# A decoder layer on one core: 16 more tokens take their first-kind expert products from gathered rows, and a fifth group of experts is worked early

## The reference, cut to what matters

```
q = h @ w_q                                   # 8 heads, two halves of 128
s = q . sub_keys                              # 128 scores for each half
top_v, eidx = best 16 of all pairs of halves  # 8 x 16 = 128 experts a token
gw = softmax(top_v)
a = gelu(h . exp_u[eidx])                     # first kind of product
out = sum over the 128 of (gw * a) * exp_v[eidx]   # second kind
```

## Time and profile before

| | |
|---|---|
| median of 3 runs | 1888.95 us (1888.36 to 1889.47) |
| the profiled execution: time, span | 1888.78 us, 1887.0 us |
| PE busy | 1846.1 us, 98% of the span |
| DVE busy | 1468.0 us, 78% |
| ACT busy | 857.3 us, 45% |
| POOL busy | 348.4 us, 18% |
| DMA | 548.22 MB, mean 291 GB/s |

### The profile page before, as it was taken

The page is one execution under the profiler, slowest core; times in us unless marked ns, Lnnn a source line. Parts: engine busy times, 40 slices in busy tenths (PEclk is TensorE's granted clock), DMA queues, the critical chain, the costliest instruction groups (busy, mean ns, idle before and its releaser), DMA issues.

```text
span 1887.0 us, 25880 instructions
## 1 busy us (share of the span) xinstructions
PE 1846.1 (98%) x10392; PEld 1620.4 (86%) x10392; DVE 1468.0 (78%) x1953; ACT 857.3 (45%) x1152; POOL 348.4 (18%) x216
## 2 busy tenths in 40 slices
PE   7999999999899999999999999999999999999997
PEld 6888888888778999997779889889889899898895
DVE  6544655576763798968898988988888989989887
ACT  5443556344533103335555455455455455455452
POOL 1000223000000000013331323232323222323210
PEclk9999999999989999999999999999999999999999
DMA  9644333846254776789999999999999999999882
GB/s 346 237 179 179 134 135 106 321 176 245 90 201 156 240 272 226 292 309 339 370 365 364 388 360 358 393 359 366 384 345 381 382 352 393 360 354 393 346 330 98
DMA packets 100199, 548.22 MB, mean 291 GB/s; under 512 B 8704, under 2 KB 33344, under 8 KB 35952
## 3 DMA queue, kind: packets, MB, share of 16 engines
q1 hardware_dynamic: 53424, 374.37, 52.5%
q0 software_dynamic: 20096, 147.04, 19.0%
q10 hardware_dynamic: 26560, 25.17, 4.3%
HBM read 530.74 MB, written 14.68 MB: 289 GB/s over the span
## 4 chain that ended last, share of the span: by engine, by line
PE 94%; DVE 3%; ACT 1%; issue 1%; DMA 0%; SPq 0%; POOL 0%; DVEq 0%; ACTq 0%
PE bank L954 16%; PE bank L581 11%; PE bank L598 9%; PE bank L855 8%; PE bank L956 7%; PE bank L887 6%; PE bank L890 6%; PE bank L886 6%; PE bank L888 6%; PE bank L889 6%; PE bank L583 6%; PE bank L875 2%; PE bank L821 1%; DVE rows L1730 1%; DVE oh L1829 1%
## 5 line engine op out<-in xcount | busy, mean ns | idle before, releaser
L581 PE MATMUL bank<-act_split,ring_hi 128*128 128x512 f32 x896 | 319.1, 399 | 10.9 <-DVE ring_lo L1362 8.2
L1840 DVE TENSOR_TENSOR split_a<-experts,split_a 128x2048 fp32r<-128x2048 f32 x124 | 283.8, 2288 | 53.5 <-ACT split_a L1277 52.8
L1351 DVE TENSOR_TENSOR ring_lo<-ring_raw,ring_hi 128x2048 fp32r<-128x2048 f32 x90 | 205.9, 2290 | 137.9 <-ACT ring_hi L1017 137.5
L1277 ACT CAST split_a<-experts 128x2048 fp32r<-128x2048 f32 x124 | 237.3, 1914 | 147.6 <-PE bank L890 146.4
L954 PE MATMUL bank<-h_split,split_a 128*128 128x384 f32 x1024 | 293.9, 359 | 0.2 <-DVE hres L1904 0.2
L956 PE MATMUL bank<-h_split,split_a 128*128 128x192 f32 x1024 | 256.3, 250 | 0.0
L583 PE MATMUL bank<-act_split,ring_lo 128*128 128x256 f32 x896 | 252.0, 281 | 0.0
L555 POOL DMA_INDIRECT rows<-in_peer_u,eidx x64 | 148.0, 2312 | 455.2 <-DVE rows L1730 452.0
L555 POOL DMA_INDIRECT rows<-in_peer_v,eidx x64 | 148.1, 2314 | 374.4 <-DVE hrow L1736 328.6
L581 PEld LDWEIGHTS bank<-act_split,ring_hi 128*128 128x128 f32 x896 | 169.5, 189 | 50.2 <-DVE act_split L1362 8.0
L1017 ACT CAST ring_hi<-ring_raw 128x2048 fp32r<-128x2048 f32 x90 | 171.8, 1909 | 83.3 <-PE bank L598 73.7
(11 more groups left out here) (295 smaller groups left out, 3457.9 us busy)
## 6 DMA issues: line engine op xcount, KB each, us to landing
experts<-in_stream SPq DMA_DIRECT2D x218, 1024.0 KB, 5.2
ring_raw<-in_stream SPq DMA_DIRECT2D x91, 1024.0 KB, 4.8
late_raw<-in_stream SPq DMA_DIRECT2D x38, 1024.0 KB
gate_matrix<-stage ACTq DMA_DIRECT2D x12, 1024.0 KB, 4.9
gbuf<-gate_matrix ACTq DMA_DIRECT2D x16, 768.0 KB, 13.3
w<-in_w SPq DMA_DIRECT2D x4, 1024.0 KB, 8.6
gb<-in_ln_g POOLq DMA_DIRECT2D x3, 1024.0 KB, 4.9
gb<-in_ln_b POOLq DMA_DIRECT2D x3, 1024.0 KB, 9.2
```

The source lines that it names most:

```text
L581: pe.matmul(bank[n % 2][:, :], hi[:, k * P:(k + 1) * P], act_split[:, k].rearrange("p c t -> p (c t)"), start=(k == 0), stop=False, skip_g ...
L1277: act.copy(split(m)[0], tile).then_inc(split_hi, 1)
L1351: dve.tensor_tensor(ring_lo[:, r, :], ring_raw[:, r, :], ring_hi[:, r, :].bitcast(F32), ALU.subtract).then_inc(lo_ready, 1)
L1840: dve.tensor_tensor(lo, raw_slot(split_slot(m))[0], hi.bitcast(F32), ALU.subtract).then_inc(split_lo, 1)
```

## The change

- `NU = 176`: the first-kind products of the early and of the late groups are made for 176 tokens in place of 192 (early 128x176; late 128x352 and 128x176). The second kind stays dense for 192.
- The other 16 tokens (176 to 191) get their first-kind products from 16 more gathers (`FIRST`; 16 x 128 rows), which stand first. They are used in the first 32 quads of the choice. Their dot products (`bpair`) get gelu on ACT at quad 33, go back by 8 small DMAs from POOL into a tile of ones (`spread_b`), and DVE multiplies them into the softmax weights at quad 38; PE transposes those again at quad 39, and ACT copies the 16 columns that changed. In `early_chunk` and `ga` the last 16 columns are set to 1 once, so that gelu(product) x gate leaves the gate for them.
- `EARLY_G = 5`: 40 early slots and 11 late groups. PE does 6 early steps a quad for 32 quads and 4 for the other 16.
- Four buffers of one-hot tiles in place of two (`HOTS`).
- Gathers: 16 during the choice, 2 while loading, 22 in V0, 10 in each late group, 4 of them in its first half.
- The first loads: x in quarters as before, but the first two weight slots in a first quarter and a rest, with the rest ahead of x's third and fourth quarter.
- The split tokens are made at chunk 31 in place of 24, and the gathered tokens' gelu at the end of its group's second half.

```diff
-EARLY_G = 4
+EARLY_G = 5
...
+NU = 176
+NB = ND - NU
+EIGHTHS = P // NB
+FIRST = PAIRS // EIGHTHS
...
+HOTS = 4
...
-STEP = 3
-CHOICE_S = 8 * EARLY_G - QUADS * STEP // KO - WHILE_LOADING
+STEPS = [6] * 32 + [4] * 16
+CHOICE_S = 8 * EARLY_G - sum(STEPS) // KO - WHILE_LOADING
+GELU_N, BACK_N, TURN_N, WEIGHTED_N = 33, 38, 39, 44
-IN_G, IN_LOADING, IN_V0, IN_LATE = 6, 2, 17, 9
-IN_LATE_U = 3
+IN_G, IN_LOADING, IN_V0, IN_LATE = FIRST, 2, 22, 10
+IN_LATE_U = 4
...  sync: the first loads
+            quarter_of_x(0)
+            for r in range(2):
+                sp.dma_start(ring_raw[:, r, 0:512], a["stream"][r][:, 0:512]).then_inc(first_landed[r], 16)
+            quarter_of_x(1)
+            for r in range(2):
+                sp.dma_start(ring_raw[:, r, 512:], a["stream"][r][:, 512:]).then_inc(landed[r], 16)
+            quarter_of_x(2)
+            quarter_of_x(3)
...  gpsimd
+            for e in range(EIGHTHS):
+                pool.dma_start(eidx_b[e * NB:(e + 1) * NB, :],
+                               eix[NU - P:NS, e * FIRST:(e + 1) * FIRST]).then_inc(eidx_landed, 16)
+            for n in range(FIRST, FIRST + 2 * GATHERS):
+                pool.wait_ge(row_used, n - BUFS + 1)
+                if n == FIRST + BUFS - 1:
+                    for half in range(2):
+                        pool.dma_start(hrow[half * NS:(half + 1) * NS, :], hres[NS:P, 1, :]).then_inc(hrow_landed, 16)
+                    pool.wait_ge(spread_ready, 1)
+                    pool.wait_ge(bpair_gelu, 1)
+                    for e in range(EIGHTHS):
+                        pool.dma_start(spread_b[NU - P:NS, e * FIRST:(e + 1) * FIRST],
+                                       bpair[e * NB:(e + 1) * NB, :]).then_inc(bpair_landed, 16)
...  tensor
-                    last = pe.matmul(bank[(N_U + k) % 2][:, 0:ND], experts[:, k % RP, ko * P:(ko + 1) * P], h2T[:, ko, :],
+                    last = pe.matmul(bank[(N_U + k) % 2][:, 0:NU], experts[:, k % RP, ko * P:(ko + 1) * P], h2T[:, ko, 0:NU],
...
+                if n == TURN_N:
+                    pe.wait_ge(weighted_ready, 1)
+                    pe.transpose(bank[2][:, 0:P], pick[:, 1, 2].rearrange("p h k -> p (h k)"), ident[:]).then_inc(idx_psum, 1)
...
-                            pe.matmul(b[:, 0:2 * ND], hi[:, w], h2_split[:, ko].rearrange("p c t -> p (c t)"), start=(ko == 0),
+                            pe.matmul(b[:, 0:2 * NU], hi[:, w], h2_split[:, ko].rearrange("p c t -> p (c t)"), start=(ko == 0),
...
-                            last = pe.matmul(b[:, 0:ND], lo[:, w], h2_split[:, ko, 0, :], start=False, stop=(ko == KO - 1),
+                            last = pe.matmul(b[:, 0:NU], lo[:, w], h2_split[:, ko, 0, :], start=False, stop=(ko == KO - 1),
...  scalar
+                if n == GELU_N:
+                    act.wait_ge(row_used, FIRST)
+                    act.activation(bpair[:], bpair[:], ACT.Gelu_apprx_tanh).then_inc(bpair_gelu, 1)
+                if n == TURN_N:
+                    act.wait_ge(idx_psum, TT + 1)
+                    act.copy(idxT[:, 2, NU:ND], bank[2][:, NU - P:NS]).then_inc(idx_out, 1)
...  vector
             for n in range(QUADS):
-                if n >= 2:
-                    dve.wait_ge(g_mm, n - 1)
+                if n >= HOTS:
+                    dve.wait_ge(g_mm, n - HOTS + 1)
+                if n == BACK_N:
+                    dve.wait_ge(spread_ready, 1)
+                    dve.wait_ge(bpair_landed, 16 * EIGHTHS)
+                    weights = pick[0:NS, 1, 2].rearrange("p h k -> p (h k)")
+                    dve.tensor_tensor(weights, weights, spread_b[0:NS, :], ALU.mult).then_inc(weighted_ready, 1)
+                if n == WEIGHTED_N:
+                    dve.wait_ge(idx_out, TT + 1)
...
-                gathers(IN_CHOICE + (IN_G - IN_CHOICE) * (n + 1) // QUADS)
+                gathers(min(IN_G, IN_G * (n + 1) // 32))
```

More of the change, by code:

```diff
@@ L275, in early_chunk @@
             flat = early[:].rearrange("p c t -> p (c t)")
-            first = 32 * T - N_EARLY * ND
-            return flat[:, first + k * ND:first + (k + 1) * ND]
+            return flat[:, k * ND:(k + 1) * ND]
         def raw_slot(n):
@@ L318, in build @@
         landed = [sem(f"landed{r}") for r in range(R)]
-        first_landed = [[sem(f"first_landed{r}{q}") for q in range(3)] + [landed[r]] for r in range(2)]
+        first_landed = [sem(f"first_landed{r}") for r in range(2)]
         first_hi = sem("first_hi")
@@ L434, in _, with quarter_of_x @@
         def _(sp):
[L435 to L436 removed]
+            def quarter_of_x(q):
+                k = slice(4 * q, 4 * q + 4)
                 sp.dma_start(act_raw[:, k, :], a["xT"][:, k, :]).then_inc(x_landed[q], 16)
[L438 to L439 removed]
+            quarter_of_x(0)
[6 more added lines that the diff above has]
+            quarter_of_x(3)
             for s in range(2, R):
@@ L874, in _ @@
                 for j in range(QUAD):
-                    last = pe.matmul(bank[4 + n % 4][:, j * P:(j + 1) * P], oh2[:, n % 2, j, :], oh1[:, n % 2, j, :],
+                    last = pe.matmul(bank[4 + n % 4][:, j * P:(j + 1) * P], oh2[:, n % HOTS, j, :], oh1[:, n % HOTS, j, :],
                                      start=True, stop=True)
                 last.then_inc(g_mm, 1)
-                for step in range(STEP * n, STEP * n + STEP):
+                if n == TURN_N:
+                    pe.wait_ge(weighted_ready, 1)
+                    pe.transpose(bank[2][:, 0:P], pick[:, 1, 2].rearrange("p h k -> p (h k)"), ident[:]).then_inc(idx_psum, 1)
+                for step in range(sum(STEPS[:n]), sum(STEPS[:n + 1])):
                     early_slot(CHOICE_S + step // KO, (step % KO, step % KO + 1))
@@ L962, in _ @@
                         for ko in range(KO):
-                            last = pe.matmul(b[:, 0:ND], tile[:, ko * P:(ko + 1) * P], h2T[:, ko, :], start=(ko == 0),
+                            last = pe.matmul(b[:, 0:NU], tile[:, ko * P:(ko + 1) * P], h2T[:, ko, 0:NU], start=(ko == 0),
                                              stop=(ko == KO - 1))
@@ L1743, in gathers @@
                 nonlocal seen
-                while seen < min(upto, 2 * GATHERS):
+                while seen < min(upto, FIRST + 2 * GATHERS):
                     gathered(seen)
```

97 lines of the change are left out of this document (58 added, 39 removed).

## The result

Six runs of the changed kernel have a median of 1878.43 us (1876.39 to 1879.41), six of the kernel before on the same chips 1889.21 us. The ratio is 0.9941, 95% interval 0.9928 to 0.9954: faster, by 0.6% or 11 us. The forecast was 1861.9 us, 27 us faster; the measured time lies inside its range of 1849 to 1879, near the upper end, and the gain is less than half of the forecast one. The profiled execution has a span of 1877.3 us against 1887.0.

What follows compares the result with a forecast made beforehand. PE's work was taken to set the time, with DMA close behind. PE's work -29.3, choice -2.8, transpose, copy and wait +1, and DMA +4 summed to -27.1 us: 1861.9 us as a median, range 1849 to 1879.

Steps and rivals of the forecast that it cites:

- V0: Stage V0: 8 chunks more at 4.60 us each, its 512-column matmuls unchanged, +36.8 us.
- Two cost 1.03 us and landed 1.7 us after: Way back of the 16 products in the choice: 5.8 us to issue and land, DVE waiting 1 to 3, unseen by PE.
- Rival 5: In the choice, the way back stalls PE by 10 us, with POOL's issues slowed: 1872 us; chance 0.05.
- rival 2: DMA becomes the bound at a 0.98 share, late groups +17 us, choice losing 8: 1879.9 us; chance 0.14.
- Early slots: Early slots at 149.7 ns a record, 4.79 us a slot, 40 in place of 32: +25.2 us.
- The pair at its floor, 271 ns: Late groups' first halves: only the wide matmul shrinks, 12.8 ns less a pair, 1.64 us a group.
- Rival 4: Late groups' pair is set by its two weight loads and doesn't shrink at all: 1875.9 us; chance 0.06.
- the bound where both shrink: Late groups: both matmuls of a pair shrink by their columns, 19.2 ns a pair, late groups -100.3 us.
- DMA, +4 us: Late groups: 71.8 us of transfers in PE's 71.6, costing 0.4 us in each of 10 groups, between 0 and 17.
- rivals 2 and 3: Rival 3: late groups' transfers go no faster than now, a group taking 76.0 us: 1902 us; chance 0.06. Rival 2: own line.
- The choice: Choice: PE and DVE run level, 3 us lost where 5 to 5.8 were: -2.8 us; extra transpose, copy, wait: +1.
- Start: First loads reordered at the kernel's start: 0 us, between -1 and +2.

Runs made afterwards that it cites:

- e1: The changed kernel with the 8 way-back DMAs issued ahead of the copies of hrow and of gathers 16 and 17 in POOL's queue: 1871.32 us.
- e2: The changed kernel without the 8 way-back DMAs and DVE's wait for them, leaving the 16 tokens' first-kind products out of its result: 1864.63 us.
- e3: The changed kernel with its three new small tiles moved behind the one-hot tiles, so w_split lies where it was before: 1869.45 us.
- e11: The kernel of e9_best with w_split alone 128 bytes higher: 1866.67 us.
- e12: The kernel of e9_best with w_split at its place and wt, gbuf and ga 128 bytes higher: 1861.90 us.
- e8: The kernel before with the fifth early group alone (EARLY_G = 5, STEP = 5, IN_V0 = 26, split tokens at chunk 29): 1889.01 us, ratio 0.9995.
- e9_best: The changed kernel with DVE's multiplication at quad 42, PE's transposes behind quad 41 and w_split at its address of before, POOL's order left: 1860.44 us.
- e7: The changed kernel with the narrow matmul of each late pair at 128 columns in place of 176: 1876.23 us.
- e4_back42: The changed kernel with DVE's multiplication at quad 42 in place of 38 and PE's transposes behind quad 41 in place of 39: 1867.15 us.

## Why the prediction was wrong

The direction it forecast was right, and so were PE's terms to within 2 us, but for V0's; the size was 27 us where 11 were measured. Two steps failed.

*"Two cost 1.03 us and landed 1.7 us after, so 4.1 + 1.7 = 5.8 us. DVE waits 1 to 3 us ... so PE doesn't see it."* The issues cost what was said, 4.28 us for eight. The landing did not: it took 11.4 us. The 1.7 us came from the indices' DMAs of the earlier trace rows, which were two of 16 KB, not eight of 1 KB, and stood in POOL's queue before any gather. Eight of 1 KB took 3.8 us even there, as the change's own indices show. On the way back they stood behind two gathers and the two copies of `hrow` (which the prediction had itself put there, and costed as POOL's time alone), while the DMA share was 1.01. e1 took both away, what was ahead and most of the traffic, and came to 4.6 us; the two were not tried apart. The rest of the passage held: DVE came to quad 38 at 820.80, and PE ran out of work 4.7 us later (834.98 - 9.46 = 825.52), the "some 5 us" of the forecast. e2 shows the price, 11.8 us before V0, of which 9.5 is idle and the rest the slower clock behind it. Rival 5 had this mechanism with its 10 us and a chance of 0.05, but for a wrong reason, slow issues.

*"V0 ... all matmuls of 512 columns, which the change leaves: +36.8."* The change left the matmuls and moved their stationary tile: three new small tiles were allocated in front of w_split. e3, e11 and e12 show that its place costs 1.3 us in V0 and 5.3 behind it, 6.6 in all. Nothing in the rows of before could have said so, but that an address moves could be read in the kernel. Of the 2.4 us that V0 missed, the other 1.1 are not the address: e8, with w_split at its place of before, also took 185.0/40 = 4.63 us a chunk and not 4.60. Why was not followed.

With the stall hidden and the address put back the forecast is met: e9_best has 1860.4 us where 1861.9 were forecast. That it comes so near is in part luck. Against the terms of the forecast it has 0.9 us more before V0, 1.1 more in V0 and 1.5 more in the late groups than PE alone was given, and the 4 us set down for DMA didn't come. It is luck too that the change itself, at 1878.4, fell inside the range and beside rival 2's 1879.9: rival 2's signs are not in its profile, where ACT waited for no slot in the late groups and DVE 0.7 us in all for rows.

The other terms, point by point:

- *Early slots* at 150 ns a record: PE's quads in the choice and the 239.2 us of e2 bear it out. The forecast had 23.4 more than before in that stretch, e2 has 239.2 - 216.0 = 23.2.
- *The pair at its floor, 271 ns*: 273 measured, so 11.2 ns less than before and not 12.8, and 1.43 us a group, not 1.64. e7 shows the floor: 48 columns fewer of the narrow matmul give at most 2.6 us of 27. That the floor is the weight load stays an argument, from the weight-load row that is busy all through the first halves. Rival 4 (no shrinking at all) is out, and so is the bound where both shrink.
- *DMA, +4 us*: nothing. At shares of 0.97 to 1.00 in ten late windows PE had no wait for a slot. With w_split in its place the late groups with the end gave 898.0 - 808.3 = 89.7, of 91.3 for PE alone. The queue could be kept full; rivals 2 and 3 had the right quantity (71.8 us of transfers in 71.6) and the wrong consequence. The Trainium skill's 358 GB/s (DMA: Bandwidth & Descriptors, section Where 436 GB/s comes from) is passed by ten of the eleven late windows, at 384 to 398 GB/s (the last has few gathers) on this one core.
- *The fifth group*: priced by the same rows at +5.1 less what PE loses in the choice, 0 to 3 expected, 0 measured. So nothing of the gain is from it by itself; that it makes room for the quads' new work is its purpose, and wasn't tried apart.
- *The choice* without the way back: of e2's 239.2 us, 190.5 are 1280 early records at 149 ns, 42.7 the quads and 0.9 the transposes; 5 are left as lost, where the forecast took 3 and 1. Its PE waited 2.0 us for one-hot tiles.
- *Start*: +0.6 in the change's profile, between -2.8 and +1.3 over all profiles, so no effect that can be told.

## What to carry to other kernels

A small transfer that something waits for can't be priced by the landing of another one in an emptier stage (1.7 us there, 11.4 here): look at the number and size of the transfers, at what is ahead of them in their own queue at that moment, and at the DMA share of that stage. Put its consumer far behind it before trying to make it faster; that was worth 10.3 us of the stretch before V0 (e4_back42), the faster landing 6.8 (e1_queue). When new tiles are allocated, look whether a stationary operand of many matmuls has moved, and if matmuls that the change doesn't touch start further apart, move it back and measure. A DMA share near 1.0 is not by itself a bound on PE: here, with rings of three to five buffers, it took nothing from PE. With shorter rings it was not tried.

## What the runs showed of the hardware

- The spacing of back-to-back matmuls of 512 columns depends on where the stationary tile lies: with w_split 216 bytes past a multiple of 256, 230.7 ns in every kernel with five early groups; 88 past one (at 182872 and at 182360), 232.6 to 232.8 ns; at a multiple of 256, 233.3 ns. That is 1% of a stage, 5 to 7 us of this kernel. Why, and what the best place is, stays open: three residues were tried. The place is not all of it: the kernel before has the 216 too, and 229.4 ns in V0.
- Eight DMAs of 1 KB, counted from the last issue to the wait's end, took 3.8 us with nothing ahead in their queue (DMA share 0.58), 4.6 us first in their queue (0.20 while they were issued, 0.94 after), and 11.4 us behind 2 MB of gathers and 1 MB of copies (1.01 and 0.93). Two of 16 KB took 1.7 us with nothing ahead.
- A narrow matmul between two wide ones costs hardly anything by its columns: the first half of a late group took 34.95 us with 176 columns, 273 ns a pair, and 34.94 or 34.52 us with 128, 273 or 270 ns. The Trainium skill (TensorE: Matmul & The Clock Gate, section LDWEIGHTS), whose load time depends on the weight columns alone, agrees with it, if the weight load is the floor.
